# Two transformer blocks with a mixture of experts: an expert stage that takes over the closing weights and half of the closing sum

## The reference, cut to what matters

```python
def expert_block(args):                     # 128 tokens of one expert
    tok_idx, e = args
    xb = t_pad[tok_idx]
    hb = xb @ w_exp_in[e] + b_exp_in[e]     # 1024 -> 2 x 1024
    g = jnp.minimum(hb[:, :D_FF], SWIGLU_LIMIT)
    u = jnp.clip(hb[:, D_FF:], -SWIGLU_LIMIT, SWIGLU_LIMIT)
    a = g * jax.nn.sigmoid(SWIGLU_ALPHA * g) * (u + 1.0)
    return a @ w_exp_out[e] + b_exp_out[e]  # 1024 -> 1024
...
y = jnp.einsum('nk,nkd->nd', gate_w, y_slot)
# then h = layer_norm(ALPHA * h + y), and the second block's x @ w_in_2
```

## Time and profile before

| what | value |
|---|---|
| median of 3 runs | 2060.29 us (2059.99 to 2060.69) |
| the profiled execution | 2060.99 us, its span 2059.2 us |
| TensorE (PE) busy | 1944.1 us, 94% of the span |
| VectorE (DVE) busy | 1610.5 us, 78% |
| ScalarE (ACT) busy | 1238.4 us, 60% |
| GpSimd (POOL) busy | 308.4 us, 15% |
| granted TensorE clock, mean | 0.976 |
| HBM | 494.43 MB read, 254 GB/s over the span |

### The profile page before, as it was taken

One profiled execution on the slowest core, in us unless ns is written; L12 is line 12 of the kernel. 1 busy time (PEld: TensorE's weight loads), 2 busy tenths in 40 slices (PEclk: granted clock), 3 DMA queues, 4 the chain that ended last, 5 costly groups with the idle time before them and its releaser, 6 DMA issues. The chain is left out here.

```text
span 2059.2 us, 28923 instructions
## 1 busy us (share of the span) xinstructions
PE 1944.1 (94%) x10108; PEld 1555.6 (76%) x10108; DVE 1610.5 (78%) x1836; ACT 1238.4 (60%) x1320; POOL 308.4 (15%) x171
## 2 busy tenths in 40 slices
PE   7979899967999999999999999999999898999898
PEld 5657688755788888888888888888888676587776
DVE  6562441476999999999999999999999674654786
ACT  3443522324777777777777777777777434653551
POOL 0102044100112112121111121111212200000100
PEclk9989999987999999999999999999999999999999
DMA  6222244446999999999999999999999742011221
GB/s 212 65 93 71 49 111 110 145 171 262 336 387 392 379 394 371 400 373 394 379 394 379 392 390 373 396 378 392 375 394 373 235 102 82 18 35 62 63 71 74
DMA packets 201644, 518.44 MB, mean 252 GB/s; under 512 B 22102, under 2 KB 81662, under 8 KB 201228
## 3 DMA queue, kind: packets, MB, share of 16 engines
q1 hardware_dynamic: 191388, 482.70, 63.1%
q0 software_dynamic: 9360, 34.08, 6.5%
q10 hardware_dynamic: 832, 0.80, 0.1%
HBM read 494.43 MB, written 28.88 MB: 254 GB/s over the span
## 5 line engine op out<-in xcount | busy, mean ns | idle before, releaser
L1882 PE MATMUL bank<-moe_upper,x_hi 128*128 128x512 f32 x1536 | 616.9, 402 | 0.3 <-DVE x_hi L2035 0.3
L1884 PE MATMUL bank<-moe_upper,x_hi 128*128 128x512 f32 x1536 | 598.9, 390 | 0.0
L1958 ACT CAST moe_upper<-beyond 128x2048 fp32r<-128x2048 f32 x192 | 367.6, 1916 | 133.1 <-PE bank L1884 128.3
L2041 DVE TENSOR_TENSOR beyond_lower<-beyond,moe_upper 128x2048 fp32r<-128x2048 f32 x192 | 434.6, 2285 | 7.6 <-ACT moe_upper L1958 5.7
L1882 PEld LDWEIGHTS bank<-moe_upper,x_hi 128*128 128x128 f32 x1536 | 288.7, 188 | 64.1 <-issue 0.7
L1884 PEld LDWEIGHTS bank<-moe_upper,x_hi 128*128 128x128 f32 x1536 | 288.4, 188 | 60.7
L1883 PE MATMUL bank<-beyond_lower,x_hi 128*128 128x512 f32 x768 | 299.5, 390 | 0.0
L1958 ACT CAST moe_upper<-mixed_t 128x2048 fp32r<-128x2048 f32 x96 | 183.9, 1915 | 77.4 <-PE bank L1884 69.3
L2041 DVE TENSOR_TENSOR mixed_t_lower<-mixed_t,moe_upper 128x2048 fp32r<-128x2048 f32 x96 | 218.1, 2285 | 10.2 <-ACT moe_upper L1958 9.6
L2041 DVE TENSOR_TENSOR above_lower<-above,moe_upper 128x2048 fp32r<-128x2048 f32 x96 | 218.1, 2286 | 5.6 <-ACT moe_upper L1958 5.6
L1958 ACT CAST moe_upper<-above 128x2048 fp32r<-128x2048 f32 x96 | 183.8, 1916 | 57.9 <-PE bank L1884 57.9
(11 more groups left out here) (623 smaller groups left out, 3418.8 us busy)
## 6 DMA issues: line engine op xcount, KB each, us to landing
beyond<-in_w_exp_in_dram SPq DMA_DIRECT2D x128, 1024.0 KB, 8.0
mixed_t<-in_w_exp_in_dram SPq DMA_DIRECT2D x64, 1024.0 KB, 7.9
above<-in_w_exp_in_dram SPq DMA_DIRECT2D x64, 1024.0 KB, 7.8
beyond<-in_w_exp_out_dram SPq DMA_DIRECT2D x64, 1024.0 KB, 8.6
mixed_t<-in_w_exp_out_dram SPq DMA_DIRECT2D x32, 1024.0 KB, 7.4
above<-in_w_exp_out_dram SPq DMA_DIRECT2D x32, 1024.0 KB, 9.3
ahead<-in_w_in_dram SPq DMA_DIRECT2D x23, 512.0 KB, 5.3
ahead<-in_w_in_dram SPq DMA_DIRECT2D x3, 1536.0 KB, 6.7
```

Of the source, the lines that this page charges most:

```text
L1882: nc.tensor.matmul(to, hi[:, f, :], upper[u][:, t, cols], start=f == 0 and not biased, stop=False)
L1884: done = nc.tensor.matmul(to, lo[:, f, :], upper[u][:, t, cols], start=False, stop=f == NK - 1)
L1958: nc.scalar.copy(upper[h % SPLIT][:, :, :], ring[s][:, :, :]).then_inc(hi_ready, 1)
L2041: nc.vector.tensor_tensor(lower[s][:, :, :], ring[s][:, :, :], upper[h % SPLIT][:, :, :].bitcast(F32), ALU.subtract).then_inc(lo_ready, 1)
```

## The change

The diff does these things:

- `merge_stage`: 1.0 is added to the half of the expert biases that belongs to u, before they are split.
- `route_stage`: the two first gathers and the waits ahead of them are taken out. `experts_stage` issues them on GpSimd after its register load.
- The sigmoid is taken from the bank by ScalarE (`gate_sigmoids`, both halves after piece 8's upper part); VectorE multiplies it by the bank (`gated`, ahead of pieces 10 and 11); `activations` is one operation, min(g, GATE_LIMIT) times the clipped u + 1, ahead of pieces 1 and 2. `gates` and `gated_input` are gone.
- First block: the second block's tokens are transposed behind the fifth piece and split into operands of their own (`second_hi`, `second_lo`). ScalarE makes the first three upper parts ahead of `tokens_hi`. The keep_busy of `first()` has four matmuls, and the transposes of the shares follow it there; VectorE splits the shares at the end of the first block.
- `last`: the second half's transposes follow the first's without keep_busy; products start when the first half of the activations is split; the outputs are computed column half by column half; share products and row products (in three-part form: y as upper and lower part) are computed here, and so are the additions of the first 512 columns. SyncE loads the closing weights and the engines split them in this stage.
- `closing_stage`: what has moved is taken out; it adds the second 512 columns with statistics between. `w1` has buffers of its own.

```diff
@@ merge_stage
             dve.wait_ge(bias_in, 48)
+            nc.vector.tensor_scalar(full[:, FF:2 * FF], full[:, FF:2 * FF], 1.0, None, ALU.add)
+            dve.drain()
@@ route_stage, gpsimd
-            pool.wait_ge(saved, v0 + 16 * NT)
-            pool.wait_ge(tokens_ready, 1)
-            for p in range(2):
-                nc.gpsimd.indirect_dma_start(
...
@@ experts_stage, sync, last
+                sp.wait_ge(x_ps, rest * 2 + 6)
+                sp.wait_ge(rows_sem[1], rest * 8 + 32)
+                for h in range(2):
+                    part = slice(4 * h, 4 * h + 4)
+                    sp.dma_start(k.ahead[:, part, 0:3 * P], column_tiles(w2, KC2, 3 * P)[:, part, :])\
...
@@ experts_stage, gpsimd
             def before():
+                for p in range(2):
+                    nc.gpsimd.indirect_dma_start(
+                        out=rows_in[p][:, :], out_offset=None, in_=k.h1[:, :],
...
+            def last(rest):
+                pool.wait_ge(w_hi, hi0 + 4)
+                close_lower(nc.gpsimd, 3)
@@ experts_stage, tensor
+                    if first and h == 4:
+                        transpose_rows(1, 16)
...
             def last(rest):
                 pe.wait_ge(x_lo_ready, rest * 2 + 6)
                 for half in range(2):
                     transpose_half(half, rest * 2 + 3 + half)
-                    keep_busy(nc, k, 0, (512, (384, 256)[half]))
+                pe.wait_ge(g_ready, rest * 2 + 4)
+                pe.wait_ge(u_ready, rest * 2 + 4)
+                for i in range(NT):
+                    share_product(i, 0)
                 pe.wait_ge(y_sb, rest * 2 + 2)
+                pe.wait_ge(a_lo_ready, rest * 2 + 3)
+                for n in (0, 1):
+                    last_products(rest, n, (0, 1), counted=True)
                 pe.wait_ge(a_lo_ready, rest * 2 + 4)
-                outputs(rest * PIECES + LAST, [slot(0, 0, n) for n in range(4)])
+                for i in (0, 1):
+                    share_product(i, 1)
+                last_products(rest, 2, (0,))
+                last_products(rest, 3, (0,)).then_inc(y_half, 1)
+                last_products(rest, 2, (1,))
+                last_products(rest, 3, (1,)).then_inc(y_half, 1)
+                pe.wait_ge(sums_ready, 3)
+                for i in range(NT):
+                    row_product(i, 0).then_inc(summed, 1)
+                pe.wait_ge(sums_ready, 4)
+                for i in range(NT):
+                    if i >= 2:
+                        share_product(i, 1)
+                    row_product(i, 1)
 
             def first():
-                keep_busy(nc, k, 5, (512,) * 6)
+                keep_busy(nc, k, 5, (512,) * 4)
+                for i in range(NT):
+                    last_share = nc.tensor.transpose(k.bank[4][0:96, i * P:(i + 1) * P],
...
@@ experts_stage, scalar
+            def gate_sigmoids(done, free):
+                act.wait_ge(used, done)
...
+                for half in range(2):
+                    nc.scalar.activation(sg2[half][:, :], k.bank[half][:, :], ACT.Sigmoid, scale=SWI).then_inc(sg_ready, 1)
...
                     if not first and h in (7, 8):
                         activations_hi(h - 7, at(q, p, 2, h - 8))
-                    if not first and h in (9, 10):
-                        gate_sigmoid(h - 9, at(q, p, 2, h - 8))
+                    if not first and h == 8:
+                        gate_sigmoids(piece(q, p, 4), at(q, p, 2))
...
@@ experts_stage, vector
+            def gated(half, ready):
+                dve.wait_ge(sg_ready, ready)
+                nc.vector.tensor_tensor(g2[half][:, :], k.bank[half][:, :], sg2[half][:, :], ALU.mult).then_inc(g_ready, 1)
...
+            def activations(half):
                 dve.drain()
+                nc.vector.scalar_tensor_tensor(out=a2[half][:, :], in0=g2[half][:, :], scalar=GATE_LIMIT,
+                                               in1=u2[half][:, :], op0=ALU.min, op1=ALU.mult).then_inc(a_ready, 1)
...
@@ experts_stage, vector, last
+                for h in range(3):
+                    dve.wait_ge(w_hi, hi0 + h + 1)
+                    close_lower(nc.vector, h)
+                    if h == 1:
+                        output_rest(0)
+                output_rest(1)
+                for i in range(NT):
+                    dve.wait_ge(r.mixed_in[i], 16)
+                    dve.wait_ge(summed, i + 1)
+                    nc.vector.tensor_tensor(k.x[:, i, 0:512], r.mixed(i)[:, 0:512], k.bank[SUM_BANKS[0][i]][:, :], ALU.add)
@@ closing_stage, vector
             for i in range(NT):
...
+                nc.vector.tensor_tensor(x[:, i, 512:D], r.mixed(i)[:, 512:D], k.bank[SUM_BANKS[1][i]][:, :], ALU.add)
+                statistics(nc, k, i, (0,))
                 dve.drain()
-                statistics(nc, k, i)
+                statistics(nc, k, i, (1,))
```

More of the change, by code:

```diff
@@ L1936, in _, with tokens_hi @@
         def _(act):
-            def tokens_hi(ready):
+            def tokens_hi(ready, hi=x_hi):
                 for half in range(2):
                     act.wait_ge(x_ps, ready + half)
-                    nc.scalar.copy(x_hi[:, 4 * half:4 * half + 4, :], k.bank[6 + half][:, :]).then_inc(x_hi_ready, 1)
+                    nc.scalar.copy(hi[:, 4 * half:4 * half + 4, :], k.bank[6 + half][:, :]).then_inc(x_hi_ready, 1)
             def output(done, free, j):
@@ L1990, in last @@
                     upper_part(slot(0, 0, n), n, rest * 24 + 48, rest * PIECES + (LAST + n - SPLIT + 1))
-                output(rest * PIECES + LAST + 4, rest + 2, rest + 1)
+                for h in range(4):
+                    if h % 2 == 0:
+                        act.wait_ge(r.close_in[h // 2], 32)
+                    part = slice(2 * h, 2 * h + 2)
+                    nc.scalar.copy(r.up[:, part, :], k.ahead[:, part, :]).then_inc(w_hi, 1)
+                act.wait_ge(y_free, rest + 2)
+                for c in range(2):
+                    act.wait_ge(y_half, c + 1)
+                    nc.scalar.activation(r.y_lower[:, 512 * c:512 * c + 512], k.bank[4 + c][:, :], ACT.Copy,
+                                         scale=r.slot_weight[:, ds(rest + 1, 1)]).then_inc(y_sb, 1)
             each_pair(act, iteration, last)
@@ L2048, in iteration @@
                 for h in range(INNER if first else PIECES):
-                    if h == INNER:
-                        gates(piece(q, p, 4))
-                    if first and h == 1:
+                    if h >= INNER + 2:
+                        gated(h - INNER - 2, at(q, p, 2, h - INNER - 1))
+                    if first and h == 2:
                         tokens_lo(1)
@@ L2064, in iteration @@
                 if first:
-                    gates(4)
                     select(at(q, 1, 1), 1)
-                    for h in range(EARLY):
-                        lower_part(piece(q, 1, h), slot(q, 1, h), h)
-                tokens_lo(at(q, p, 2, 3))
+                    lower_part(piece(q, 1, 0), slot(q, 1, 0), 0)
+                    tokens_lo(3, second_hi, second_lo)
+                    for half in range(2):
+                        gated(half, half + 1)
+                    for h in range(1, EARLY):
+                        lower_part(piece(q, 1, h), slot(q, 1, h), h)
+                else:
+                    tokens_lo(at(q, p, 2, 3))
+                if first:
+                    dve.wait_ge(share_ps, 1)
+                    nc.vector.tensor_copy(share_t, k.bank[4][0:96, :])
+                    dve.drain()
+                    split_lower(nc.vector, k.bank[4][LOWER_SHARE, :], share_t[LOWER_SHARE, :], share_t[LOWER_SHARE, :])\
+                        .then_inc(sums_ready, 1)
             def last(rest):
@@ L2073, in last @@
                 for half in range(2):
-                    gated_input(half)
-                    activations(half, rest * 2 + 3 + half)
+                    activations(half)
                 lower_part(rest * PIECES + LAST, slot(0, 0, 0), 0)
```

176 lines of the change are left out of this document (75 added, 101 removed).

## The result

The changed kernel takes 2043.99 us (median of 4 runs, 2042.11 to 2045.06), beside 2060.49 us for the kernel before in the same session: a ratio of 0.9917, 95% interval 0.9900 to 0.9934. The profiled span fell from 2059.2 to 2040.9 us.

What follows compares the result with a forecast made beforehand. TensorE was taken to bound the expert loop, with gains at its two ends. The terms -5.3 - 1.2 + 0.5 - 2.8 + 0.6 + 2.2 - 7.0 + 0.3 = -12.7 us took 2060.3 to 2047.6; range 2043.6 to 2052.6.

Steps and rivals of the forecast that it cites:

- Step 1: End of the route stage: without the gathers GpSimd's drain shortens and the barrier falls 5.3 us earlier.
- Steps 2 and 3: Barrier to first product: shorter fill, net 1.2 us less; first gather perhaps late, 0.5 us charged.
- Step 4: Start of the second block: tokens ready sooner, 2.8 us less; a late VectorE lower part gives 0.6 back.
- Step 5: Expert loop: two sigmoids ahead of piece 9 delay the token transposes, 0.07 us per block, 2.2 us more.
- loop free of delay: Rival for the expert loop: the slack holds, no delay per block, total 2045.4 us; chance 0.14.
- Step 6: Behind the loop, up to the aggregation: products start earlier and the aggregation comes 7.0 us sooner.
- Step 7: Merge stage: the added operation pushes VectorE's bias splits further under GpSimd's; 0.3 us more, between 0 and 3.7.
- From there on all is as before: Everything from the aggregation on: no change, 0 us.

Runs made afterwards that it cites:

- two doses: The changed kernel with an extra sigmoid in each block, 128x512 or 128x128: ratios to the kernel before 0.9983 and 0.9926.
- small dose: The changed kernel with an extra sigmoid of 128x128 in each block, 0.17 us start to start: ratio to the kernel before 0.9926.
- large one: The changed kernel with an extra sigmoid of 128x512 in each block, 0.48 us start to start: ratio to the kernel before 0.9983.
- gathers_back: The changed kernel with the first two gathers issued at the end of the route stage again: ratio to the kernel before 0.9953.
- gathers_only: The kernel before with only the first two gathers moved to the start of the expert stage: ratio to the kernel before 0.9986.
- merge_bare: The changed kernel without the operation adding 1 to the experts' input biases in the merge stage: ratio to the kernel before 0.9909.
- fetch_back: The changed kernel with three more 128-column fill matmuls in the closing stage: ratio to the kernel before 0.9921.

## Why the prediction was right or wrong

- **Bound and direction: right.** TensorE bounds the loop, the gains lie at the two ends.
- **Step 1: right**, 4.9 of 5.3; undone, the drain was back.
- **Steps 2 and 3: right in kind, 1.7 too small.** The gather landed 4.4 us after its issue and 0.4 ahead of its transposes, so the 0.5 that I charged was not due. The rest is the clock: I left five fill instructions at half clock, and it rose earlier, behind an idle time of 1.8 us and not 6.7. Of ten kernels with the fill of four and the gathers in this stage, six reached the product at 9.06 to 9.26 and four at 10.68 to 10.77. My 10.6 was the slow case, and that both profiles of the changed kernel met the fast one is luck; what decides between them is not shown.
- **Step 4: right**, 2.3 against 2.2 net, with the new wait (0.50) where I had put it.
- **Step 5: the term that failed**, "so 0.07 of slack against 0.11 to 0.19 of delay". The delay came about (piece 9 started when the sigmoids ended, 0.08 us later than before), but the two doses show 0.11 of slack still left behind it, so there had been some 0.2. I had taken the gap between the split's end and the weight load as the slack; the weight load stands 0.23 us ahead of its matmul before, 0.20 in the changed kernel, 0.03 with the small dose and 0.01 with the large one, so it can slip by most of that before the matmul moves. The rival "loop free of delay" held: 0.44 in place of 2.2. Half of the looped blocks take 35.39 in place of 35.36; what that 0.03 is stays open.
- **Step 6: right in kind, 1.5 too large.** I counted "two closing splits" on VectorE ahead of the second remainder; there are three, and the third runs beside GpSimd's. The remainder was ready 16.55 us behind the loop's end, not 15.3. That is one half; the other is the clock, which I left high: TensorE's row products began at 14.84 with its dip, 13.76 in gathers_back without it, and with the dip TensorE's own work reaches the aggregation at 27.5 as well. Of ten profiles with GpSimd's split and without a fall of the clock at the loop's very end, five had the dip and five had not, and all lie at 27.50 to 27.61. The Trainium skill ("SBUF — State Buffer", section "SBUF: two separate sides") says that VectorE's operation with two SBUF inputs and a GpSimd operation that reads SBUF exclude each other for a whole instruction. The trace agrees: VectorE's split ended 1.07 us behind GpSimd's end in the changed kernel (1622.79 and 1621.72) and 1.08 behind it in gathers_back, though it had started 0.7 us earlier against the loop's end; the remainder beside it, which reads a bank, took its usual 0.75.
- **Step 7: right in size (+0.4) by luck, and its far end is real.** The 0.4 hangs on one profile of the kernel before, 185.11 us. Its other profile took 185.80, gathers_only 185.86 and merge_bare 185.87, against 185.76 to 186.01 with the operation: outside the long case it costs 0.1 or nothing. I had bounded the step at 3.7 (its own terms, 0.8 + 4.3 - 1.8, give 3.3) and set that aside as an unlikely end. It is a case of its own, with a price of 6 us, in 3 of 10 profiles. It lasts as long as GpSimd's split: the copy ended 0.03 us behind its end (285.83 and 285.80). I had looked for it at the bias splits, and it stands at a copy of two columns 2.4 us behind the last of them.
- **Put at nothing: all that lies behind the aggregation** ("From there on all is as before"). The gates' stage is 1.7 us shorter, and fetch_back takes 1.4 of that away again by three matmuls of fill in the closing stage. The stretch behind the aggregation is 0.8 shorter, and why stays open. The clock is part of it at most: its slow stretch ended 6.9 and 3.8 us behind the aggregation in the two profiles of before (59.23 and 58.68 us) and 4.4 in those of the changed kernel (58.17), so the profile with the earliest end still took 0.5 us longer.

The misses in order: gates' stage 1.7, loop 1.8, start 1.7, closing stage's end 0.8, step 4 0.1; the other way, steps 1 and 7 together 0.5 and step 6 1.5. That makes the 4.1 between the forecast and the table's sum.

## What to carry to other kernels

Where a chain ends in a weight load, measure its slack by a dose in the chain, not by the gap to the load. When work is moved behind a loop, list every instruction of each engine's queue up to the end, and look for a GpSimd operation beside VectorE's: the 1.1 us at the end (where the clock stays high) and the 6 us in the merge stage both came from one. Where two chains end together, as TensorE's and VectorE's do behind this loop, shortening one shows only in the executions in which it is the later. A gap removed can be worth more than its length, since TensorE's clock may fall behind it (1.6 us at the second block, in two profiles of four that had the gap), and for the same reason one part of a change may show less than its place in the whole.

## What the hardware did that I had not expected

- GpSimd arrives at this barrier only when its gathers have landed: 10.12 us of drain, which ended at 480.2 where the second gather landed at 480.1. The drain is gone with them and was back, 10.29 us, in gathers_back.
- A VectorE copy of 128x2 elements took 4.48 us in place of 0.16 when it started 0.10 to 0.15 us behind GpSimd's split of 4.6 us. That is no general threshold: in the changed kernel's last part VectorE's second closing split started 0.10 us behind GpSimd's (1618.24 and 1618.14) and took its usual 1.22.
- A 16 KB packet of instructions (1.07 us) among a load's packets goes with a landing 1.05 us later. A few instructions more or less on one engine move it, and with it a change gained 1.7 us and an edit lost 1.4 in a stage that neither touches.
- TensorE leaves this loop 2.2 us after its last matmul in both kernels. Before, the trace names VectorE's `moe_a` as what ended the wait; in the changed kernel that had ended at 1604.84, 2.07 us ahead of TensorE's start, the gap is as long, and the trace names nothing. The hardware loop has eight rounds there that do no work. That they are the cause was not tried.
